# A hybrid trunk's expert layers on one core: where the overflow branch stands, a row block of one expert in two idle buffers, and down slots given back in halves

## The reference

```python
for l in range(DEPTH):                      # 2 layers
    h = rms_norm(x, norm1_g[l])
    proj = h @ w_in[l]
    ...                                      # state-space branch and attention, mixed
    x = x + mixed @ w_out[l]
    h2 = rms_norm(x, norm2_g[l])
    # each token: 2 of 32 experts
    #   (silu(gt) * up) @ w_down[e],  gt, up = split(h2 @ w_gate_up[e])
    x = x + hier_moe(h2, router_w_group[l], ..., w_gate_up[l], w_down[l])
```

## Time and profile before

| | |
|---|---|
| median of three runs | 1317.05 us |
| the profiled execution | 1316.96 us, of it a span of 1315.1 us from the first to the last instruction |
| TensorE busy | 1124.5 us (86% of the span) |
| VectorE, ScalarE, GpSimd busy | 32%, 15%, 13% |
| HBM read | 460.73 MB, 351 GB/s over the span |
| mean granted TensorE clock | 0.934 |

### The profile page before, as it was taken

How to read it: one execution, slowest core, us unless ns; L and a number is a source line. 1 busy time by engine, 2 the same in 40 slices (tenths; PEclk the granted TensorE clock), 3 DMA queues, 4 the chain that set the end, 5 groups by cost and what they waited for, 6 DMA issues and landing times.

```text
span 1315.1 us, 17981 instructions
## 1 busy us (share of the span) xinstructions
PE 1124.5 (86%) x7434; PEld 509.5 (39%) x7435; DVE 417.9 (32%) x859; ACT 199.6 (15%) x439; POOL 165.5 (13%) x186
## 2 busy tenths in 40 slices
PE   9999999999766696569899999999996766775697
PEld 6445546433321232123264455464332312331232
DVE  5799733311100111011185996232111101110111
ACT  4423404000000000000054224030000000000000
POOL 1767300000000000000044762000000000000000
PEclk9999999999978897789999999999998878987899
DMA  8533687999999999999974326979999999999997
GB/s 275 184 129 129 256 343 298 383 426 428 434 428 426 431 435 428 425 430 424 404 219 170 126 88 256 391 275 424 423 428 433 431 431 426 435 431 428 425 421 302
DMA packets 61985, 462.72 MB, mean 352 GB/s; under 512 B 20488, under 2 KB 20704, under 8 KB 40416
## 3 DMA queue, kind: packets, MB, share of 16 engines
q1 hardware_dynamic: 60880, 461.70, 85.0%
q10 hardware_dynamic: 1040, 0.09, 0.1%
HBM read 460.73 MB, written 1.05 MB: 351 GB/s over the span
## 4 chain that ended last, share of the span: by engine, by line
PE 66%; DMA 28%; SPq 3%; issue 1%; DVE 1%; ACT 1%; DVEq 0%
DMA pool_all<-in_w_gate_up_dram 26%; PE ps L1135 23%; PE ps L857 9%; PE ps L1151 4%; PE ps L891 4%; PE ps L731 4%; PE ps L916 3%; PE ps L1050 2%; PE ps L1082 2%; PE ps L710 2%; PE ps L741 2%; PE ps L872 2%; DMA pool_all<-in_w_down_dram 2%; SPq L538 2%; SPq L634 2%; PE ps L775 1%
## 5 line engine op out<-in xcount | busy, mean ns | idle before, releaser
L1135 PE MATMUL ps<-pool_all,xs 128*32 128x512 f32 (+1 forms) x2816 | 332.5, 631 | 158.6 <-DMA pool_all<-in_w_gate_up_dram 157.0
L1135 PEld LDWEIGHTS ps<-pool_all,xs 128*32 128x32 f32 x2816 | 91.7, 116 | 391.9 <-issue 389.7
L1151 PE MATMUL ps<-pool_all,early 128*32 128x512 f32 (+1 forms) x1408 | 160.3, 605 | 23.0 <-ACT early L1487 13.4
L1941 DVE SCALAR_TENSOR_TENSOR rope<-rope,ps 128x512 f32<-128x512 f32 x22 | 15.1, 687 | 505.7 <-ACT rope L1485 505.7
L857 PE MATMUL ps<-pool_all,hT 128*128 128x512 f32 x256 | 114.6, 598 | 0.0
L1485 ACT ACTIVATE rope<-ps 128x512 f32<-128x512 f32 x22 | 13.1, 597 | 626.6 <-PE ps L1135 626.6
L1151 PEld LDWEIGHTS ps<-pool_all,early 128*32 128x32 f32 x1408 | 44.9, 111 | 123.9 <-issue 121.2
L2230 POOL TENSOR_TENSOR pool_all<-pool_all 128x512 f32<-128x512 f32 x64 | 79.8, 1278 | 37.3 <-DVE pool_all L1717 37.3
L1082 PE MATMUL ps<-xs,cst 128*128 128x512 f32 x176 | 81.4, 605 | 0.0
L1050 PEld LDWEIGHTS ps<-cst,hT 128*128 128x128 f32 x640 | 73.0, 192 | 16.8 <-issue 16.8
L1050 PE MATMUL ps<-cst,hT 128*128 128x128 f32 x640 | 76.8, 278 | 0.0
(11 more groups left out here) (262 smaller groups left out, 1020.0 us busy)
## 6 DMA issues: line engine op xcount, KB each, us to landing
pool_all<-in_w_gate_up_dram SPq DMA_DIRECT2D x38, 4096.0 KB, 27.7
pool_all<-in_w_down_dram SPq DMA_DIRECT2D x58, 2048.0 KB, 21.8
pool_all<-in_w_gate_up_dram SPq DMA_DIRECT2D x34, 2048.0 KB, 15.6
pool_all<-in_w_in_dram SPq DMA_DIRECT2D x12, 2048.0 KB, 11.4
pool_all<-in_w_gate_up_dram SPq DMA_DIRECT2D x24, 1024.0 KB, 11.8
pool_all<-in_w_gate_up_dram SPq DMA_DIRECT2D x24, 512.0 KB, 12.7
pool_all<-in_w_glu_dram SPq DMA_DIRECT2D x4, 2048.0 KB, 10.8
pool_all<-in_w_out_dram SPq DMA_DIRECT2D x4, 2048.0 KB, 12.1
```

Source lines behind the costliest of these rows:

```text
L1135: mm = pe.matmul(ps[r, half], xT[:, k // 4, k % 4, r], lane_cols(n, h, k % 4, half), start=(k == 0), stop=(k == KC - 1), skip_group_check= ...
L1151: mm = pe.matmul(ps[r, 2 + half], ffT[:, c, r], lane_cols(n, 2, c, half), start=(c == 0), stop=(c == 3), skip_group_check=True)
```

## The change

It has three parts.

1. `BRANCH` goes from 8 to 10: units 8 and 9 are now the loop's fourth pass on TensorE (and the last two passes on ScalarE and VectorE), and the branch on `ov_flag` stands between unit 9 and unit 10 on every engine.
2. Row block 0 of part 0 of expert 2 no longer goes to slot 6. Its two column halves go to `early` and `rope_cols` (`load_corner`), and unit 0 reads them there (`first_lanes`). Row block 0 of slot 6 is loaded in the front with what it has to hold for unit 1, so the first group of pieces after `freed` has two pieces instead of three. The load of slot 10 is cut in two halves, with a wait on `mid_std` and the second corner between them.
3. Unit 0 raises `freed` a fourth time after row block 1 of its down's second half; the three down loads of unit 1 are cut into halves, and the first halves wait for that.

```diff
@@ -61,7 +61,7 @@
-BRANCH = UNITS - 3
+BRANCH = UNITS - 1
@@ -325,6 +325,7 @@
+    corner = early, rope_cols
@@ -345,10 +346,10 @@
-    freed = signal("freed", 3)
+    freed = signal("freed", 4)
@@ -464,6 +465,13 @@
+            def load_corner(half, index):
+
+                sp.dma_start(corner[half], expert_part(index, 0)[:, 0, 512 * half:512 * half + 512]).then_inc(landed[6], 16)
@@ -515,7 +523,8 @@
-            load_part(6, l * EXPERTS + 2, 0)
+            load_piece(6, l * EXPERTS + 2, 0, 1, 4, landed[6])
+            load_piece(6, l * EXPERTS + TRIO + 2, 0, 0, 1, landed[6])
@@ -528,16 +537,19 @@
             load_part(7, l * EXPERTS + 2, 1)
             load_part(8, l * EXPERTS + 2, 2)
-            for part in range(2):
-                sp.wait_ge(front_used, at(front_used, l, 7 + part))
-                sp.sem_inc(settled, 1)
-                load_part(9 + part, l * EXPERTS + DUO, part)
+            load_corner(0, l * EXPERTS + 2)
+            sp.wait_ge(front_used, at(front_used, l, 7))
+            load_part(9, duo, 0)
+            sp.wait_ge(front_used, at(front_used, l, 8))
+            load_piece(10, duo, 1, 0, 2, landed[10])
+            sp.wait_ge(mid_std, at(mid_std, l, NT))
+            load_corner(1, l * EXPERTS + 2)
+            load_piece(10, duo, 1, 2, 4, landed[10])
@@ -545,11 +557,16 @@
-                    load_piece(part_slot(part, e), index, part, a, b, landed[part_slot(part, e)])
-            sp.wait_ge(unit_used, at(unit_used, l, 3))
-            sp.sem_inc(settled, 1)
-            for e, index in ((0, duo), (1, duo + 1), (2, second + 2)):
-                load_part(part_slot(2, e), index, 2)
+                    if (n, e) != (0, 2):
+                        load_piece(part_slot(part, e), index, part, a, b, landed[part_slot(part, e)])
+            for half in range(2):
+                if half:
+                    sp.wait_ge(unit_used, at(unit_used, l, 3))
+                else:
+                    sp.wait_ge(freed, at(freed, l, 4))
+                sp.sem_inc(settled, 1)
+                for e, index in ((0, duo), (1, duo + 1), (2, second + 2)):
+                    load_piece(part_slot(2, e), index, 2, 2 * half, 2 * half + 2, landed[part_slot(2, e)])
@@ -586,7 +603,6 @@
             for u in range(4, BRANCH):
                 load_home(u, 0 if u % 2 else 9)
                 load_rest(u)
-            load_home(BRANCH, 9)
             sp.wait_ge(routed, at(routed, l, 1))
@@ -607,9 +623,6 @@
             sp.nop()
-            load_rest(BRANCH)
-            load_home(UNITS - 2, 0)
-            load_rest(UNITS - 2)
             last = l * EXPERTS + (UNITS - 2) * TRIO
@@ -1152,6 +1165,8 @@
+                    if first and c == 1 and half:
+                        mm.then_inc(freed, 1)
@@ -1210,6 +1225,8 @@
             def first_lanes(n, part, k, half):
+                if n == TRIO and part == 0 and k == 0:
+                    return corner[half]
@@ -1250,8 +1267,6 @@
             pe.nop()
-            unit(BRANCH, TRIO, trio_lanes(BRANCH - 1, away=True), turn=BRANCH // 2, away=True)
-            unit(BRANCH + 1, TRIO, trio_lanes(BRANCH), turn=BRANCH // 2)
             unit(UNITS - 1, TRIO, trio_lanes(UNITS - 2, away=True), last=True, turn=UNITS // 2, away=True)
```

More of the change, by code:

```diff
@@ L347, in trunk @@
     front_loads = [3, 3, 3, 2, 0, 0, 0, 0, 0, 1, 1]
-    unit_loads = [8, 3, UNITS - 1, UNITS + 1, 4, UNITS - 1, UNITS + 1, 4, UNITS - 2, UNITS // 2 + 1, 2]
+    unit_loads = [8, 3, UNITS, UNITS + 1, 4, UNITS, UNITS + 3, 4, UNITS - 1, UNITS // 2 + 1, 3]
     landed = [signal(f"landed{i}", 16 * (front_loads[i] + unit_loads[i])) for i in range(RING + 2)]
     tail_in = [signal(f"tail_in{n}", TRIO * 16) for n in range(7)]
-    freed = signal("freed", 3)
+    freed = signal("freed", 4)
     ov_landed = signal("ov_landed", 16 * 6 * OV_PAIRS)
@@ L466, in load_part, with load_piece @@
                 sp.dma_start(wide_slot(i), expert_part(index, part)).then_inc(landed[i], 16)
+            def load_piece(i, index, part, a, b, sem):
+                sp.dma_start(wide_slot(i)[:, a:b], expert_part(index, part)[:, a:b]).then_inc(sem, 16)
+            def load_corner(half, index):
+                sp.dma_start(corner[half], expert_part(index, 0)[:, 0, 512 * half:512 * half + 512]).then_inc(landed[6], 16)
             def load_pair(i, index):
@@ L530, in _ @@
             load_part(8, l * EXPERTS + 2, 2)
-            for part in range(2):
-                sp.wait_ge(front_used, at(front_used, l, 7 + part))
-                sp.sem_inc(settled, 1)
-                load_part(9 + part, l * EXPERTS + DUO, part)
-            def load_piece(i, index, part, a, b, sem):
-                sp.dma_start(wide_slot(i)[:, a:b], expert_part(index, part)[:, a:b]).then_inc(sem, 16)
-            duo, second = l * EXPERTS + DUO, l * EXPERTS + TRIO
+            load_corner(0, l * EXPERTS + 2)
+            duo, second = l * EXPERTS + DUO, l * EXPERTS + TRIO
+            sp.wait_ge(front_used, at(front_used, l, 7))
+            sp.sem_inc(settled, 1)
+            load_part(9, duo, 0)
+            sp.wait_ge(front_used, at(front_used, l, 8))
+            sp.sem_inc(settled, 1)
+            load_piece(10, duo, 1, 0, 2, landed[10])
+            sp.wait_ge(mid_std, at(mid_std, l, NT))
+            load_corner(1, l * EXPERTS + 2)
+            load_piece(10, duo, 1, 2, 4, landed[10])
             for n, (part, a, b) in enumerate(((0, 0, 1), (0, 1, 2), (0, 2, 4), (1, 0, 2), (1, 2, 4))):
@@ L1093, in arrived @@
                     if first:
-                        for slot in ((0, 3, 6), (4, 7), (2, 5, 8))[part]:
-                            landed_by(slot, 1)
+                        for slot, loads in (((0, 1), (3, 1), (6, 4)), ((4, 1), (7, 1)), ((2, 1), (5, 1), (8, 1)))[part]:
+                            landed_by(slot, loads)
                     elif experts == 2:
-                        for slot, loads in (((9, 1), (0, 4)), ((10, 1), (1, 2)), ((2, 2), (5, 2)))[part]:
+                        for slot, loads in (((9, 1), (0, 4)), ((10, 2), (1, 2)), ((2, 3), (5, 3)))[part]:
                             landed_by(slot, loads)
@@ L1101, in arrived @@
                         landed_by(3, 2, i)
-                        landed_by(6, 2, i)
+                        landed_by(6, 4, i)
                     elif part == 1:
-                        landed_by(10 if away else 1, 2 if away else 3)
+                        landed_by(10 if away else 1, 3)
                         landed_by(4, 3 if away else 4)
@@ L1107, in arrived @@
                     else:
-                        landed_by(2, 1, i)
-                        landed_by(5, 1, i)
-                        landed_by(8, 0, i)
+                        landed_by(2, 2, i)
+                        landed_by(5, 2, i)
+                        landed_by(8, 1, i)
                 def tail(n):
@@ L1507, in _ @@
             act.nop()
-            main_unit(BRANCH)
-            main_unit(BRANCH + 1)
             main_unit(UNITS - 1)
@@ L2154, in _ @@
             ve.nop()
-            inner_unit(BRANCH)
-            inner_unit(BRANCH + 1)
             if l < DEPTH - 1:
```

## The result

The changed kernel takes 1321.29 us (median of seven runs, 1319.53 to 1324.55), the kernel before 1316.87 us (seven runs, 1316.44 to 1317.36). The ratio of the means is 1.0039, 95% interval 1.0029 to 1.0049 (the medians alone give 1.0034): slower by 0.4%. The prediction's time was 1.6 us above before, the medians lie 4.4 us apart; its likeliest class was no measurable difference, and by its own threshold of 1319.7 us this is slower (chance 0.24). The profiled execution took 1322.51 us with a span of 1320.7 us, 5.6 us more than before. The runs of the changed kernel lie 5.0 us apart, those of before 0.9.

A forecast was written before the change was run, and what follows sets the result against it. Transfers at 431 GB/s were taken to set the loop's pace, TensorE waiting at every unit. Layer 0 +2.2 and layer 1 -0.63 made +1.6 us on the profiled 1316.96, with 0.09 for the median 1318.6; range 1315.0 to 1321.8.

The forecast's parts named there:

- The branch row: TensorE's branch between units 9 and 10: long in layer 0, some 6.8 us (0.65); short in layer 1, 0.3 us (0.75).
- the mechanism in layer 0: Long branch readies unit 10 7.3 us after unit 9's scatter, then half clock slows its gate and up: layer +2.2 us.
- With a short branch 0.8 us are covered: Unit 10's DMA waits (0.78 + 1.38 + 0.95 us) hide a short branch, so the layer ends with the transfers: -0.63 us.
- unit 10 is ready at 625.38 + 7.3 - (0.63 + 1.43): Layer 0: unit 9's data and scatter come earlier by both gains, so unit 10 is ready at 630.6 us.
- +2.2: Layer 0's end with a long branch: 657.4 us against 655.19 before.
- The 1.43 us: Extra load time around the old branch, put to code fetches; expected two units later, with 0 gain at the layer's end.
- the long interval: Between ends of gate and up loads where TensorE passes the old branch: 45.31 us against 43.89, once per layer.
- The corners and halves: Two corners loaded early gain 1.23 us per layer, less 0.4 for a gap and 0.2 for finer down loads: -0.63 us.
- The gap forecast near 236 us: DMA queue runs dry at 235.7 us, the next group's flow begins at 236.1: 0.4 us lost, bounds 0.3 to 0.7.
- The cases: One branch long, one short 1318.6 (0.50); both short 1315.8 (0.24); both long 1321.5 (0.16); both short without 1.43 us 1313.0 (0.10).
- case 3: Both layers' branches long, TensorE stalled in front of unit 10: 2 x 2.2 = +4.4 us, 1321.5, chance 0.16.
- both branches would be long: Reading of the 256-instruction block rule: the skipped body exceeds a block, so both jumps fetch; layer 1's 0.33 us disagreed.

The follow-up runs named there:

- part 1 alone: Kernel before with only BRANCH moved from 8 to 10, units 8 and 9 in the loops, no corners or halves: 1321.54 us, ratio 1.0037.
- part 1 without the body: Kernel before with BRANCH moved to 10 and TensorE's overflow body left out, no corners or halves: 1316.58 us, ratio 0.9998.
- the kernel before without its body: Kernel before with TensorE's overflow body left out, BRANCH still at 8: 1316.94 us, ratio 0.9999.
- parts 2 and 3 together: Changed kernel with BRANCH back at 8 and units 8 and 9 written out again: 1316.72 us, ratio 0.9997.
- the last kernel: Changed kernel with 110 dead instructions jumped over in each loop pass, 8 for the test, 20 dead in layer 0's body: 1325.27 us, ratio 1.0063.

## Why the prediction was right and wrong

**The branch row** was right in both layers: 6.2 and 0.33 us, forecast 6.8 and 0.3. So was the mechanism in layer 0: unit 10 ready 6.95 us behind the scatter (7.3 forecast), its gate and up 15.8 us at the lowered clock (15.4), 4.2 us to its down (4.3), and no DMA wait left. That layer 1's stayed short was luck in part: nothing in the prediction told where its code would lie, and 64 instructions more made it 6.05 us.

**The step that failed first** is "With a short branch 0.8 us are covered ... and the layer's end goes with the transfers: -0.63 us". I took the 0.33 us of the row for the whole price of a short branch. The row of before couldn't show the rest, for behind it TensorE waited for weights anyway: as I read the traces, a short branch only means that the block of code with the target is there, and the next is fetched from then on, ready some 6 us after the jump. With six matmuls left in the target's block, 2.16 us of it are seen, and the idle time pulled the clock down behind it. In place of -0.63 layer 1 measured +1.5 in the changed kernel's profile (+2.4 for the branch and unit 10), and 0.0 in that of part 1 alone, where the clock stayed up. The +1.5 is 2.1 us beyond the forecast.

**The second** is "unit 10 is ready at 625.38 + 7.3 - (0.63 + 1.43)". The two gains were to bring unit 9's scatter forward by 2.06 us; it came 0.21 us earlier. The 1.85 us between the two are nearly all of the 1.9 by which layer 0 went beyond its +2.2 (measured +4.1). The weights were there 1.38 us sooner, but unit 9 used the time up. Unit 7, 8 and 9's gate and up, before:

```profile
504.85:520.74 15.89, 15.89 (x129) 4.27 (x129) 0.00 (x0) 0.00 (x0) 0.00 (x0) 0.87 1.02 434
550.29:565.65 15.36, 15.36 (x129) 4.15 (x129) 0.00 (x0) 0.00 (x0) 0.00 (x0) 0.90 1.03 438
594.17:609.78 15.61, 15.61 (x129) 4.17 (x129) 0.00 (x0) 0.00 (x0) 0.00 (x0) 0.89 1.01 427
```

and in the changed kernel:

```profile
505.06:520.96 15.90, 15.90 (x129) 4.23 (x129) 0.00 (x0) 0.00 (x0) 0.00 (x0) 0.87 1.03 440
548.89:565.06 16.17, 16.17 (x129) 4.31 (x129) 0.00 (x0) 0.00 (x0) 0.00 (x0) 0.86 1.03 441
592.77:609.19 16.42, 16.42 (x129) 4.31 (x129) 0.00 (x0) 0.00 (x0) 0.00 (x0) 0.85 1.01 428
```

The same 128 matmuls take 0.8 us more in unit 8 and again in unit 9, at a granted clock of 0.86 and 0.85 in the place of 0.90 and 0.89. From unit to unit at an even 43.88 us the duration grows by a quarter of a microsecond, and the longer interval of before had set it back by half a microsecond. Another 0.4 us go in the loop's form of the unit: ahead of unit 9's down TensorE waits 0.92 us for ScalarE, 0.54 before. That these eat the 1.38 us is read from the traces; that nothing is left at the end is measured (part 1 without the body, 0.9998).

**The 1.43 us**, forecast to come back later in the layer, did: the last pieces of layer 1 land 3.3 us later than before where the units ahead of them ran 2.0 us later. I had put the long interval to fetches of code, and the traces bear this out in the main: in the kernel before without its body the interval at this place is 43.87 us and the next one is long. In the ten kernels with `BRANCH` at 10 no 16 KiB packet of code falls between 400 and 620 us, and there every load lands at an even pace; each long interval of the others has such a packet in it. But such packets also pass without a late load (six between 264 and 345 us of the kernel before), so how one makes a load late stays open.

**The corners and halves** were forecast at -0.63 us per layer; the profiled execution shows -0.22 and -0.48 up to unit 7, and parts 2 and 3 together measure 0.9997. The gap forecast near 236 us is there:

```profile
234.00:235.00 1.00, 1.00 (x12) 0.26 (x8) 0.00 (x0) 0.00 (x0) 0.00 (x0) 1.00 1.00 406
235.00:236.00 1.00, 1.00 (x16) 0.34 (x12) 0.00 (x0) 0.00 (x0) 0.00 (x0) 1.00 1.14 430
236.00:237.00 1.00, 1.00 (x16) 0.31 (x12) 0.00 (x0) 0.00 (x0) 0.00 (x0) 1.00 0.82 238
```

In the last of these microseconds 238 instead of some 420 GB/s moved (410 there before), 0.43 us of transfers, as reckoned. The gap was right; the two layers gave 0.22 and 0.48 us where 0.63 each was forecast, and the whole is too small to be measured.

**The cases.** The time fell on that of case 3, "both branches long", by another way: one long, one short with a stall of its own. A stall that begins after the branch was in none of the cases. That the range held the time is luck, for its upper end was made for that case; the forecast was +1.6 us in the place of +4.4. In the five kernels with both branches long the time is 1325 to 1330 us, not 1321.5, though each of them has added instructions.

The prediction read the rule of the Trainium skill ("Runtime: NRT & Kernel Launch", "Instruction fetch mechanics") as "both branches would be long". The section says that a taken branch forces a fetch when its target isn't in the current window of two blocks, so a jump over more than one block can still be short, as layer 1's was. The traces agree with the rule's kind: jumps over some 10 and 215 instructions (counted from the program) bring no stall, one over 470 stalls 6 us or not, and 64 instructions turn layer 1's from one into the other. The packets of code are 16 KiB, as its blocks are. That a block is 256 instructions could not be confirmed here, since the last kernel went against my count by it. And a window of two blocks is not what holds the loop: two passes of 1041 recorded instructions, over four such blocks each, ran without a packet of code.

## What to carry to other kernels

A branch over code that never runs isn't free: where the code at its target wasn't at hand, TensorE stood for 6 us with a saturated DMA, and came back at half clock. Leave it where the engine waits for data anyway, or make what is jumped over short. Where a row shows a short branch under a wait, look for what the wait hides behind it. And data that come 1.4 us earlier need not make the end earlier: here 0.8 us of it went in slower matmuls, with the granted clock at 0.85 in the place of 0.89.

## What the runs showed of the hardware

Code that never runs changed the time: 64 dead instructions made a kernel of 1321.3 us one of 1328.6. The loop's 1041 recorded TensorE instructions per pass ran on without an instruction packet from 352 to 533 us, though layer 0's jump over 470 waited for one. A wait for code ended 1.35 to 1.62 us behind the end of its 16 KiB packet, 19 times of 19. In the traces with long branches the stall was 4.8 to 7.5 us, and a further stall (1.41 us in the kernel with 64 dead instructions), or the clock falling behind a 2.2 us stall or not (16.69 against 13.92 us for the same 122 matmuls), comes on top. That such differences make the wide spread of the changed kernel's runs (5.0 us, against 0.9 before) is likely, but each kernel has one trace only, and it isn't shown.
